# Compressed pages turned by VectorE in 32 x 32 squares, gathered by quarter blocks

## What is computed

```python
CMP_LEN, CMP_STRIDE = 32, 16
# rows: [tokens, 2, heads, 64]; block m covers tokens 16 m to 16 m + 31
hidden[c] = silu(sum over token t of 32: rows[16 m + t, c, h, :] @ cmp_w1[c, t] + cmp_b1[c])   # 64 -> 128
out[c]    = hidden[c] @ cmp_w2[c]                                                              # 128 -> 64
# keys (c = 0) are then normed and rotated; queries attend to them, and the
# probabilities pick the 16 best blocks of 64 tokens for the selected branch
```

## Time and profile before

| | |
|---|---|
| median of 3 runs | 2079.4 us (2075.82 to 2081.9) |
| span of the profiled execution | 2075.2 us (the page shows no other time of it) |
| TensorE busy | 1912.7 us (92%) |
| VectorE, ScalarE, GpSimd busy | 712.8, 473.6, 227.0 us |
| prompt stage | about 1320 to 1543 us of the span |
| sample stage | about 1545 to 2000 us of the span |

### The profile page before, as it was taken

One profiled execution on the slowest core, in us unless ns is written; L12 is line 12 of the kernel. 1 busy time (PEld: TensorE's weight loads), 2 busy tenths in 40 slices (PEclk: granted clock), 3 DMA queues, 4 the chain that ended last, 5 costly groups with the idle time before them and its releaser, 6 DMA issues. The chain is left out here.

```text
span 2075.2 us, 26135 instructions
## 1 busy us (share of the span) xinstructions
PE 1912.7 (92%) x9695; PEld 1154.3 (56%) x9695; DVE 712.8 (34%) x1620; ACT 473.6 (23%) x1032; POOL 227.0 (11%) x333
## 2 busy tenths in 40 slices
PE   5779999999999999997989999789889999999878
PEld 3345645564655565456864448655555555555467
DVE  3213232323242423240121314167652444444332
ACT  1311211211131112110011011246442333333310
POOL 0000100010001000100000000024352112111000
PEclk8879999999999999998999999779899999999989
DMA  9942561355135422635121236500024444443431
GB/s 299 387 155 72 201 215 43 120 180 187 43 143 183 162 80 106 229 116 219 41 81 41 81 59 245 169 26 2 1 79 186 177 179 173 182 178 123 138 88 43
DMA packets 119388, 281.79 MB, mean 136 GB/s; under 512 B 33320, under 2 KB 41966, under 8 KB 115543
## 3 DMA queue, kind: packets, MB, share of 16 engines
q1 hardware_dynamic: 101100, 170.57, 24.7%
q0 software_dynamic: 12928, 109.54, 13.2%
q10 hardware_dynamic: 5268, 0.36, 0.3%
HBM read 227.79 MB, written 60.86 MB: 139 GB/s over the span
## 5 line engine op out<-in xcount | busy, mean ns | idle before, releaser
L2187 PE MATMUL sample_bank<-area 128*128 128x508 f32 x512 | 234.3, 600 | 4.8 <-DVE area L2428 4.8
L1080 DVE SCALAR_TENSOR_TENSOR mlstm_cring<-mlstm_cring,mlstm_cur_old,mlstm_bank 128x512 f32<-128x512 f32 x128 | 87.1, 743 | 223.4 <-PE mlstm_bank L842 223.4
L2187 PEld LDWEIGHTS sample_bank<-area 128*128 128x128 f32 x512 | 92.0, 190 | 106.6 <-issue 98.7
L1368 PE MATMUL proj_bank<-stage,area 128*128 128x512 f32 x320 | 142.4, 603 | 6.3 <-ACT area L1445 6.3
L760 PE MATMUL mlstm_bank<-h,stage 128*128 128x272 f32 x512 | 126.7, 411 | 15.4 <-issue 10.9
L760 PEld LDWEIGHTS mlstm_bank<-h,stage 128*128 128x128 f32 x512 | 102.0, 200 | 39.3 <-issue 12.6
L815 PE MATMUL mlstm_bank<-h,stage 128*128 128x272 f32 x512 | 121.2, 395 | 0.0
L826 PE MATMUL mlstm_bank<-stage,h 128*128 128x512 f32 x256 | 114.1, 599 | 0.0
L815 PEld LDWEIGHTS mlstm_bank<-h,stage 128*128 128x128 f32 x512 | 96.0, 190 | 27.9 <-issue 9.1
L777 PE MATMUL mlstm_bank<-stage,h 128*128 128x512 f32 x256 | 110.9, 594 | 0.0
L1368 PEld LDWEIGHTS proj_bank<-stage,area 128*128 128x128 f32 x320 | 60.9, 193 | 87.5 <-issue 85.9
(11 more groups left out here) (513 smaller groups left out, 2709.1 us busy)
## 6 DMA issues: line engine op xcount, KB each, us to landing
stage<-in_a_w_in SPq DMA_DIRECT2D x16, 2048.0 KB, 8.9
mlstm_cring<-in_state_C SPq DMA_DIRECT2D x32, 1024.0 KB, 5.5
o_Cs<-mlstm_cring POOLq DMA_DIRECT2D x32, 1024.0 KB, 4.7
stage<-in_a_ada_w SPq DMA_DIRECT2D x4, 2048.0 KB, 12.6
sample_winr<-in_cache_kv_win SPq DMA_DIRECT2D x8, 1024.0 KB, 5.3
o_win_s<-in_cache_kv_win SPq DMA_DIRECT2D x1, 8128.0 KB
stage<-in_w_kv SPq DMA_DIRECT2D x3, 2048.0 KB, 7.7
act_scratch<-mlstm_szt POOLq DMA_DIRECT2D x4, 1088.0 KB, 8.3
```

The lines of the kernel that those rows point to most:

```text
L1080: dve.scalar_tensor_tensor(c, c, cur_old[:, n:n + 1], bank[:, b_big("outer", n * KH + k), :], ALU.mult, ALU.add).then_inc(E["c_new"], 1)
L1368: last = pe.matmul(o, h[:, k, a * P:(a + 1) * P], w[:, k, :], start=(k == 0), stop=(k == KD - 1))
L2187: t = pe.matmul(out, S.w1[:, c, o * 8 + k, :], xt[:, k, :, o:o + M - 1], start=(k == 0 and o == 0), stop=(k == 7 and o == 1))
```

## The change

The rows are gathered in quarter blocks: 4 tokens of 512 numbers, 8 KB, per partition. Partition 32 a + r of tile t holds quarter a of block 32 t + r. In this layout a 32 x 32 turn inside each group of 32 partitions gives the operand of the products at once: VectorE turns 128 x 1024 numbers per instruction, from the staging area straight into `xt`. The rows of `cmp_w1` are loaded in the order that this layout asks for. One sequence is 4 gathers and 2 x 4 turns. `pieces`, the identity products, their evictions and GpSimd's copies are gone, `xt` has a buffer for each half, and the fills that are left (`FILLS` = 14 per sequence) are counted anew. The prompt's rows are one tile, with two turns.

```diff
 phase_project (SP)
-            for ch in range(2 * BKV):
-                sp.dma_start(rows[:, ch, :].rearrange("m (p d) -> m p d", d=BD), src[:, :, ch, :]).then_inc(E["rows_in"], 16)
+            src = I["o_cmp_p"].rearrange("o (m a q) c h d -> a m (o q c h d)", a=4, q=4)
+            for a in range(4):
+                sp.dma_start(S.stage[32 * a:32 * a + 32, 0:QUARTER], src[a]).then_inc(E["rows_in"], 16)
 helpers
+def load_w1(sp, I, w1, c, loaded):
+    src = I["cmp_w1"][c].rearrange("(s a q) (b d) e -> s a d (q b) e", s=2, a=4, b=2)
+    for s in range(2):
+        for a in range(4):
+            sp.dma_start(w1[32 * a:32 * a + 32, c, 8 * s:8 * s + 8, :], src[s, a]).then_inc(loaded, 16)
+def turn_blocks(dve, tile, xt, c, M, t):
+    src = tile.rearrange("p (q x) -> p q x", q=4)[:, :, c * BKV * BD:(c + 1) * BKV * BD]
+    out = flat(xt, "pqhbm").rearrange("p (j m) -> p j m", m=M)[:, :, 32 * t:32 * t + 32]
+    return dve.transpose(out, src)
+def load_quarters(pool, I, blk, t, name, out, loaded):
+    src = I[name].rearrange("g (r q) c h d -> (g r) (q c h d)", q=4)
+    pool.indirect_dma_start(out, None, src, bass.IndirectOffsetOnAxis(ap=blk[:, t:t + 1], axis=0)).then_inc(loaded, 16)
 phase_prompt
+                load_w1(sp, I, S.w1, c, E[f"w_in{c}"])          # SP; w2 and the gain follow, then the spill
+            for a in range(4):                                  # SP, behind the 8 DMAs of S.blocks
+                for j in range(4):
+                    at = 32 * a + 8 * j
+                    sp.dma_start(S.quarters[at:at + 8, :, :], four[j].partition_broadcast(8),
+                                 allow_slow_non_contiguous=True).then_inc(E["page_in"], 16)
-            pool.wait_ge(E["page_in"], 16 * (PAGE // CST))
+            pool.wait_ge(E["page_in"], 16 * (PAGE // CST + 16))
-            pool.wait_ge(E["xt_tr"], 16)
-            load_blocks(pool, I, S.blk, "cache_kv_cmp", S.stage[:, :], E["rows_in"])
+            pool.wait_ge(E["xt_ok"], 2)
+            for t in range(4):
+                load_quarters(pool, I, S.blk, t, "cache_kv_cmp", S.stage[:, t * QUARTER:(t + 1) * QUARTER], E["rows_in"])
+            for c in range(2):                                  # VectorE, in place of compress_dve's evictions
+                turn_blocks(dve, S.stage[:, 0:QUARTER], xt[:, c], c, M, 0).then_inc(E["xt_ok"], 1)
 phase_sample, GpSimd
             def next_rows(m):
+                hold(pool, E["xt_ok"], m * 2, E["pass_pool"])
+                for t in range(4):
+                    load_quarters(pool, I, S.blk, t, "cache_kv_cmp", S.stage[:, t * QUARTER:(t + 1) * QUARTER], E["rows_in"])
+            next_rows(1)
+            with pool.Fori(1, NS - 1) as n:
+                hold(pool, E["rows_in"], n * 64, E["pass_pool"])
+                next_rows(n + 1)
+                next_sel(n)
 phase_sample, TensorE
             def products(m, c, ks):
                 if ks[0] == 0:
+                    pe.wait_ge(E["xt_ok"], m * 2 + c + 1)
-                if with_next:
-                    turn_pieces(seg, n + 1, 1)
 phase_sample, VectorE
+            def blocks_out(m, c, ts):
+                if ts[0] == 0:
+                    dve.wait_ge(E["hid_mm"], m * 2 - 1 + c)
+                    if c == 0:
+                        dve.wait_ge(E["rows_in"], m * 64)
+                for t in ts:
+                    last = turn_blocks(dve, S.stage[:, t * QUARTER:(t + 1) * QUARTER], xt[c], c, M, t)
+                if ts[-1] == 3:
+                    last.then_inc(E["xt_ok"], 1)
 ...
+                if next_c1:
+                    blocks_out(n + 1, 1, (0, 1))       # behind keys_out 6, before the maximum L2463
 ...
+                if next_c1:
+                    blocks_out(n + 1, 1, (2, 3))       # behind keys_out 10, before L2473
 ...
+                if next_c0:
+                    blocks_out(n + 2, 0, (0, 1, 2, 3)) # behind the maximum L2493, before the copy L2498
 ...
+            blocks_out(1, 0, (0, 1, 2, 3))             # before the loop, behind the eight turns of sequence 0
+            with dve.Fori(0, NS - 2) as n:
+                attend(n, True, True)
+            attend(NS - 2, True, False)
+            attend(NS - 1, False, False)
```

More of the change, by code:

```diff
@@ L1549, in _ @@
                 dve.drain().then_inc(E["q_done"], 1)
[L1552 to L1588, removed]
@@ L1591, in compress_act @@
[L1591 to L1609, removed]
@@ L1612, in compress_dve @@
[L1612 to L1635, removed]
@@ new lines, in compress_products @@
+def compress_products(pe, w1, xt, c, k, out, M):
+    for o in range(2):
+        last = pe.matmul(out, w1[:, c, o * 8 + k, :], xt[:, k // 2, :, k % 2, o:o + M - 1], start=(k == 0 and o == 0),
+                         stop=(k == 7 and o == 1))
+    return last
+def load_quarters(pool, I, blk, t, name, out, loaded):
+    src = I[name].rearrange("g (r q) c h d -> (g r) (q c h d)", q=4)
+    pool.indirect_dma_start(out, None, src, bass.IndirectOffsetOnAxis(ap=blk[:, t:t + 1], axis=0)).then_inc(loaded, 16)
@@ L1978, in _, with turned_at, out_a_at, out_d_at @@
                     copy_out(u - 3)
[L1981 to L1998, removed]
+FILLS = 14
+FILLS_ON_ACT = (0, 1, 3, 5, 7, 9, 11, 13)
+ON_ACT = len(FILLS_ON_ACT)
+def turned_at(n, j):
+    return n * FILLS + j + 1
+def out_a_at(n, j):
+    return n * ON_ACT + 1 + len([f for f in range(j + 1) if f in FILLS_ON_ACT])
+def out_d_at(n, j):
+    return n * (FILLS - ON_ACT) + 1 + len([f for f in range(j + 1) if f not in FILLS_ON_ACT])
 def phase_sample(nc, I, S):
@@ L2010, in phase_sample @@
         HW = WIN // 2
-        rows = S.stage[:, :].rearrange("p (a c) -> p a c", a=CST)
-        pieces = sb("pieces", [P, BKV, CST * BD])
+        xt1 = sb("xt1", [P, 8 * BKV * M])
+        xt = [x.rearrange("p (q h b m) -> p q h b m", q=4, h=BKV, b=2) for x in (S.spare[:, 0:8 * BKV * M], xt1[:, :])]
         sel = sb("sel", [P, NPG, KV2])
         winr = sb("winr", [P, TT, KV2])
-        xt = S.spare[:, 0:8 * BKV * M].rearrange("p (k h m) -> p k h m", k=8, h=BKV)
         ktw = sb("ktw", [P, 2, WIN])
@@ L2168, in turn_pieces @@
-            def turn_pieces(seg, m, c):
-                for i in range(8):
-                    p, half = c * BKV + i // 2, i % 2
-                    j = i if c == 0 else 19 + i
-                    room(seg, j)
-                    if half == 0:
-                        pe.wait_ge(E["piece_ok"], m * (2 * BKV) + p + 1)
-                    for q in range(4):
-                        k = half * 4 + q
-                        t = pe.transpose(bank[:, j % 3, q * M:(q + 1) * M], pieces[:, p % BKV, k * P:(k + 1) * P], ident)
-                    t.then_inc(E["turned"], 1)
@@ L2318, in attend @@
                 fill_in(1, [4, 5, 6, 7])
[L2320 to L2323 removed]
+            products(0, 0, range(8))
+            products(0, 1, range(8))
             with pe.Fori(0, NS - 1) as n:
[L2325 to L2327 removed]
+                attend(n, True)
+            attend(NS - 1, False)
             hold(pe, E["o2_ok"], NS + 1, E["pass_pe"])
@@ L2539, in _ @@
             dve.drain()
-            pieces_out(first[0], 0, 0)
-            pieces_out(first[0], 0, 1)
-            with dve.Fori(0, NS - 1) as n:
-                pieces_out(both(n), n + 1, 0)
-                attend(both(n), n, True)
-            attend(last, NS - 1, False)
+            dve.sem_inc(E["out_d"], 1)
+            for c in range(2):
+                for t in range(4):
+                    last = turn_blocks(dve, S.stage[:, t * QUARTER:(t + 1) * QUARTER], xt[c], c, M, t)
+                last.then_inc(E["xt_ok"], 1)
+            blocks_out(1, 0, (0, 1, 2, 3))
[3 more added lines that the diff above has]
+            attend(NS - 1, False, False)
             dve.drain()
```

288 lines of the change are left out of this document (122 added, 166 removed).

## The result

The changed kernel takes 2116.47 us (median of 4 runs, 2115.83 to 2120.28) against 2078.95 us beside it (4 runs, 2075.82 to 2081.90): a ratio of 1.0188, 95% interval 1.0169 to 1.0206. It is slower by 1.9%, and 5.5 us above the 2111 us forecast. The profiled execution took 2116.52 us with a span of 2114.9, 39.7 more than before's 2075.2.

What follows compares the result with a forecast made beforehand. TensorE, 92% busy, was taken to bound the loop. Terms +37.4 - 3.0 - 9.8 + 7 = +31.6 us took the span from 2075.2 to 2106.8; with 4.2 to the median, 2111 us, range 2085 to 2145.

Steps and rivals of the forecast that it cites:

- from there to the first output products: Start of the sample stage: VectorE's turns let the first output products come at 1581.1 instead of 1590.91, -9.8 us.
- six sequences: Sample stage, sequences that gather ahead: each 58.6 us in place of 52.4, +37.4 us over six.
- seventh: Seventh sequence of the sample stage turns but gathers nothing: -4.4 + 1.4 = -3.0 us.
- One sign: Listed as showing the forecast right: the first output products of the sample stage come about 10 us sooner.
- The turn: VectorE turn of 128 x 1024 fp32 at one pass: 1.22 us, eight per sequence.
- rival 1: A turn of fp32 on VectorE takes two passes, 2.39 us, giving 2178 us in all; chance 0.14.
- The staging area and the gather: Per sequence, t from output products' start: second turn pair frees staging area at 23.0, gather takes 13.3 us, lands at 36.9.
- rival 3: Sample stage: four gathers spread better, land in 9.5 us, TensorE keeps its clock; about 2079 us; chance 0.14.
- What waits behind it: Four VectorE turns, then the copy freeing TensorE's L2297 (L2220 after) at t = 42.2; TensorE stands for 10.5 us.
- Clock and end of the sequence: After L2297: 14.0 us of work, plus 1.6 for TensorE's lower clock after the stand and 0.8 waiting for SiLU.
- First pair: Turns on VectorE ahead of the compressed scores' maximum take 2.44 us, of which 1.4 reach TensorE; bounds 0 to 2.44.
- Prompt stage: SP's longer load queue delays page numbers, GpSimd's first weighing and TensorE's first turn of probabilities: +7 us.

Runs made afterwards that it cites:

- The first two experiments: Changed kernel with the four waiting turns moved behind VectorE's coefficients: 2039.67 us; changed kernel with only one of four gathers per sequence issued: 2059.66 us.
- the last two experiments: Changed kernel with three moves of turns and page numbers, plus output weights issued ahead of the last window (2017.99 us) or behind the last selected rows (2009.15 us).
- the page-number experiment: Changed kernel with GpSimd taking up the prompt's page numbers and four gathers after its first weighing instead of before: 2097.78 us, ratio 1.0101 to the kernel before.

## Why the prediction was right

The sum was +31.6 us and the span grew by 39.7; the medians grew by 37.5. The two differ because before's profiled execution was a quick one: in every run on record the time lies 1.6 to 1.8 us above the span, so its 2075.2 stands for some 2077, about 2 us under the median. Term by term, from starts in the two traces:

| stretch | predicted | measured |
|---|---|---|
| start of the prompt stage (SyncE's first load, 1319.64, now 1321.67) | 0 | +2.0 |
| prompt stage, to VectorE's first fill of the sample stage (225.3, now 234.7) | +7 | +9.5 |
| from there to the first output products (46.0, now 35.2) | -9.8 | -10.8 |
| six sequences (52.4 each, now 59.2) | +37.4 | +40.7 |
| seventh (49.4, now 46.3) | -3.0 | -3.1 |
| eighth (47.7, now 49.5) | 0 | +1.9 |
| output stage | 0 | -0.4 |

No large miss hid another: +3.3 us in the six sequences, +2.5 in the prompt stage, +2.0 ahead of it and +1.9 in the eighth sequence stand against -1.0 at the start of the sample stage. One sign did not show as written: in the span's own time the first output products came at 1591.58, against 1590.91 before, since the late prompt stage used up the 10.8 us that the start of the sample stage gained.

*The turn.* 1.22 us taken, 1.214 measured, so rival 1 (2.39) fell. By the Trainium skill (Vector Engine (DVE) Microarchitecture Reference, The reshape front-end and per-opcode configuration) a turn keeps one element per cycle and lane; the prediction's estimate of 1.24 us, which rests on it in part, agrees with the row.

*The staging area and the gather.* The second pair was forecast to end at t = 23.0 and the rows to land at 36.9; in the third sequence it was 22.6 and 37.3. The landing was 13.9 us after the first issue where 13.3 was taken. Four transfers of 1 MB did not land sooner than one of 4 MB, so rival 3's 9.5 us fell. The Trainium skill's line (DMA: Bandwidth & Descriptors, Anatomy of one DMA, SWDGE path), an estimated 11.6 us for these bytes, is again too short here; the trace decides. At the start of the stage the second sequence's rows landed at 1587.0, not at about 1572: 11.5 us of that is the later stage, and GpSimd issued the first of the four gathers only at 1572.74, 6.6 us after the staging area came free; what held it no row names. It cost nothing, by a narrow margin: the turns ended 1.7 us before the products that need them (1593.40).

*What waits behind it.* L2220 was forecast at t = 42.2 behind a stand of 10.5 us. Over the six sequences it came at 41.9 to 42.7, mean 42.2, behind stands of 10.3 to 11.1. The first two experiments hold it from both sides: with the other order the stand goes, with a quarter of the bytes it shrinks to 2.3 to 3.0. The products that the prediction counts ahead of the stand are four, not two (eight records); no term hangs on it.

*Clock and end of the sequence: the term mis-sized.* From L2220 to the next output products 14.0 + 1.6 + 0.8 = 16.4 us were forecast. The seventh sequence, which gathers nothing and does not stand, takes 14.81 (1978.16 to 1992.97), so the 14.0 and the 0.8 hold. The six, from the same two starts, take 17.6, 16.6, 16.3, 17.8, 17.0 and 16.4, mean 16.9. Nearly all of the difference lies in the eight records of products behind L2220 (5.0 to 6.6 us in place of 3.67), whose first 3 us have a granted clock of 0.50 each time: the clock costs 1.5 to 3.0 us behind a stand, 2.1 on average where 1.6 was taken. That is 6 x 0.5 = 3.2 of the 3.3 us by which the sequences were dearer. The row behind the 1.6 lay at the low end of what follows a long stand.

*First pair.* 1.4 us was taken between bounds of 0 and 2.44; L2187 came at t = 17.0 (17.3 forecast) behind a wait of 1.14.

*Prompt stage.* The mechanism was right, the size short by 2.5 us. SyncE's timeline of the kernel after:
```profile
1321.96 8.12 SPq L1558 DMA_DIRECT2D area<-in_cmp_w  x16
...
1339.45 16.72 SPq L1659 DMA_DIRECT2D quarters<-in_page_table  x16
```
and GpSimd's there:
```profile
1361.40 0.27 POOL L1679 TENSOR_SCALAR blocks<-blocks,const 128x8 int32<-128x8 int32 x1 [19.96 <-DMA quarters<-in_page_table]
...
1368.15 3.24 POOL L1697 TENSOR_SCALAR x<-x,prompt_coef,gnat 128x128 f32<-128x128 f32 x6
```
The weights' loads issued in 0.51 us each (0.63 taken), the quarters' page numbers in 1.05 (0.71 taken; for the sixteen, 11.4 us taken and 16.7 measured). The cheaper weights nearly cancelled the 2.0 us ahead of the stage as far as the first quarter load (1339.45, forecast 1340), and the quarters' issues then cost 5.3 us more: landed at 1361.4, not 1356.4. From landing to the first weighing it took 6.75 us (5.8 forecast). TensorE's first turn of the probabilities came 12.9 us later than before, 5.9 more than the forecast 7; 2.0 of it lie ahead of the stage, and 1.4 were made up behind.

*What was not forecast.* The eighth sequence waits 6.18 us for its selected rows in place of 3.39; in the last two experiments the same wait follows the output weights that are moved beside it. Why it grew between the two kernels no run isolates: it was 4.3 us and 6.2 in two profiles of one and the same kernel. The 2.0 us ahead of the prompt stage were 0.8 in another kernel with the same code there (1320.46 at the page-number experiment), and stay open.

## What to carry to other kernels

When a transfer's buffer is freed late, the engine that consumes it will wait, and what that costs is decided by what stands behind the wait in that engine's program: here the wait for the same late gather cost 77 us ahead of a 0.24 us copy that TensorE needs, and TensorE stood for none of it once the copy went first. So list, for each wait that a change adds, the instructions of the same engine that follow it and do not need it, and put those first. The same reading of GpSimd's queue found 19 us. On SyncE 6 us came from another question: which transfers move beside the one that is waited for.

## What the runs showed of the hardware that was not expected

- Loads differ in the time that their issue takes, and not by their bytes. The issues by line of the kernel after (ns minimum, median, maximum):
```profile
L1558 SPq DMA_DIRECT2D area<-in_cmp_w x16: 312/450/617, 1322.0 to 1329.6; - x16
```
```profile
L1654 SPq DMA_DIRECT2D blocks<-in_page_table x8: 600/625/1392, 1332.0 to 1338.8; - x8
```
```profile
L1659 SPq DMA_DIRECT2D quarters<-in_page_table x16: 351/1088/1953, 1339.5 to 1355.1; - x16
```
The hidden weights, 128 KB each, issue fastest; the quarters' page numbers, 1 KB each, take more than twice that. What sets it was not tried.
- The clock falls behind some stands and not behind others of the same length: with a quarter of the bytes, 2.28 and 2.44 us cost nothing, 2.32 and 2.46 cost 1.7. Behind 10 to 11 us it fell each time, and cost between 1.5 and 3.0 us. What tells them apart was not tried.
- Four gathers of 1 MB, issued 1.25 us apart, land each 8.3 us after its own issue in the median, but in the third sequence the last is there only 13.9 us after the first issue: no sooner than one gather of 4 MB (13.3).
